# Attention's transposes placed one product later, the last means placed inside half products, and the last output pieces divided anew

## The reference, cut to what matters

```python
# NoPE differential attention: 4 heads, two 64-wide q/k maps each, 128-wide values
s = jnp.einsum('bqhcd,bkhcd->bhcqk', q, k).astype(jnp.float32)
s = jnp.where(mask, s, -jnp.inf)                  # block-causal mask, prompt only
p = jax.nn.softmax(s, axis=-1)
wdiff = p[:, :, 0] - lam * p[:, :, 1]
o = jnp.einsum('bhqk,bkhe->bqhe', wdiff, v)
yc = rmsnorm(o, da_g) * (1.0 - lam_init)
...
x = x + (jax.nn.silu(upc[..., :D_FF]) * upc[..., D_FF:]) @ w_dn    # D_FF = 2816
y = rmsnorm(x, norm_f)                                             # the output
```

## Time and profile before

| what | value |
|---|---|
| median of 3 runs | 1000.32 us (999.03 to 1001.5) |
| profiled execution, its own time | 1000.77 us |
| its span (first to last instruction and transfer) | 999.0 us |
| PE busy | 975.5 us (98%) |
| DVE busy | 692.0 us (69%) |
| ACT busy | 473.0 us (47%) |
| POOL busy | 161.2 us (16%) |
| mean granted TensorE clock | 0.996 |

### The profile page before, as it was taken

How to read it: one execution, slowest core, us unless ns; L and a number is a source line. 1 busy time by engine, 2 the same in 40 slices (tenths; PEclk the granted TensorE clock), 3 DMA queues, 4 the chain that set the end, 5 groups by cost and what they waited for, 6 DMA issues and landing times.

```text
span 999.0 us, 20129 instructions
## 1 busy us (share of the span) xinstructions
PE 975.5 (98%) x7763; PEld 952.6 (95%) x7763; DVE 692.0 (69%) x1161; ACT 473.0 (47%) x982; POOL 161.2 (16%) x343
## 2 busy tenths in 40 slices
PE   7999999999999998999999999999999999999996
PEld 6999899999999998999999999999999999999996
DVE  6887666687667898777775547777777777533353
ACT  5675555576555665655553433333333333322241
POOL 2000121110121221121112211111121111111000
PEclk9999999999999999999999999999999999999998
DMA  6522243364231222233244222222222223323342
GB/s 196 196 85 86 77 107 108 99 212 126 64 86 49 80 86 85 65 97 95 80 142 144 85 73 93 89 85 86 85 85 86 85 85 101 117 83 86 90 132 90
DMA packets 104086, 99.87 MB, mean 100 GB/s; under 512 B 4868, under 2 KB 99481, under 8 KB 103735
## 3 DMA queue, kind: packets, MB, share of 16 engines
q1 hardware_dynamic: 98799, 85.51, 28.0%
q10 hardware_dynamic: 4072, 10.23, 2.9%
q0 software_dynamic: 1120, 2.86, 1.0%
HBM read 91.26 MB, written 7.31 MB: 99 GB/s over the span
## 4 chain that ended last, share of the span: by engine, by line
PE 85%; DVE 6%; issue 4%; ACT 4%; POOL 1%; DMA 0%; DVEq 0%; POOLq 0%; ACTq 0%
PE D L1719 46%; PE D L1776 28%; PE D L1736 2%; DVE w_l L1305 2%; ACT w_h L1009 1%; PE X L1988 1%; PE X L2026 1%; PE D L1828 1%; PE D L1748 1%; DVE ups L1675 1%; PE D L1880 1%; PE X L1934 1%; DVE acc L1685 0%; PE X L1935 0%; PE X L1937 0%
## 5 line engine op out<-in xcount | busy, mean ns | idle before, releaser
L1305 DVE TENSOR_TENSOR w_l<-raw,w_h 128x512 fp32r<-128x512 f32 (+1 forms) x286 | 201.0, 720 | 111.2 <-ACT w_h L1009 109.4
L1776 PE MATMUL D<-a_h,w_h 128*128 128x272 f32 x840 | 250.4, 298 | 3.0 <-DVE tmp L1486 1.6
L1776 PE MATMUL D<-a_h,w_l 128*128 128x272 f32 x840 | 243.0, 289 | 0.0
L1776 PE MATMUL D<-a_l,w_h 128*128 128x272 f32 x840 | 241.6, 288 | 0.0
L1009 ACT ACTIVATE w_h<-raw 128x512 fp32r<-128x512 f32 (+1 forms) x286 | 171.5, 618 | 101.0 <-PE D L1719 77.8
L1776 PEld LDWEIGHTS D<-a_h,w_h 128*128 128x128 f32 x840 | 158.1, 188 | 8.4 <-DVE tmp L1486 3.0
L1776 PEld LDWEIGHTS D<-a_l,w_h 128*128 128x128 f32 x840 | 158.4, 189 | 0.0
L1776 PEld LDWEIGHTS D<-a_h,w_l 128*128 128x128 f32 x840 | 158.0, 188 | 0.0
L1719 PE MATMUL D<-h_h,w_h 128*128 128x272 f32 x704 | 145.9, 288 | 0.1
L1719 PE MATMUL D<-h_h,w_l 128*128 128x272 f32 x704 | 145.7, 288 | 0.0
L1719 PE MATMUL D<-h_l,w_h 128*128 128x272 f32 x704 | 145.1, 288 | 0.0
(11 more groups left out here) (346 smaller groups left out, 1676.8 us busy)
## 6 DMA issues: line engine op xcount, KB each, us to landing
raw<-in_w_in SPq DMA_DIRECT2D x64, 512.0 KB, 4.3
raw<-in_w_up SPq DMA_DIRECT2D x44, 512.0 KB, 4.3
raw<-in_w_down SPq DMA_DIRECT2D x20, 512.0 KB, 3.8
raw<-in_w_branch SPq DMA_DIRECT2D x12, 512.0 KB, 3.6
raw<-in_w_out SPq DMA_DIRECT2D x8, 512.0 KB, 4.2
raw<-in_w_down SPq DMA_DIRECT2D x10, 384.0 KB, 3.4
x_spill<-xT ACTq DMA_DIRECT2D x1, 2176.0 KB, 7.4
xT<-x_spill ACTq DMA_DIRECT2D x1, 2176.0 KB, 10.5
```

The lines of the kernel that those rows point to most:

```text
L1305: v.tensor_tensor(split_view(w_l, g), whole_view(g), split_view(w_h, g).bitcast(F32), ALU.subtract)\
L1776: last = t.matmul(out, wt[:, k, :], x[:, left, k, :], start=w in (1, 2, 5) and k == i == 0, stop=k == KQ - 1 and i == 2, skip_group_check= ...
```

## The change

Three edits.

1. In attention the sub-steps `t`, `wt`, `o`, `sq`, `rr`, `on`, `y`, `yt` and `yc` are filed one tick later. `s`, `mx`, `ex` and `wd` stay.
2. PE's mean 0 is issued in the middle of half block (6, 1), ahead of k tile 11 of 22, and mean 1 in the middle of half block (7, 1). DVE's two small steps of mean 1 stand behind the drain of (7, 1) now, no longer ahead of `scale` 0.
3. The last pieces: DVE scales rows c = 2 in two halves, the right half of rows c = 3, and the right half of the sample rows; ACT scales the left half of rows c = 3 and the left half of the sample rows. SP sends the first three, ACT the left half of c = 3 and the sample rows.

```diff
@@ -136,8 +136,8 @@
         at_time(time, *step)
     for u in range(17):
         t0, t1 = (99 + 28 * (x // 4) + (0, 5, 11, 18)[x % 4] if x >= 0 else 91 for x in (u - 1, u))
-        for dt, sub in ((0, "s"), (1, "mx"), (2, "ex"), (3, "wd"), (5.5, "t"), (6.5, "wt"), (8, "o"), (9, "sq"),
-                        (9, "rr"), (11.5, "on"), (t1 - t0 + 8, "y"), (t1 - t0 + 9, "yt"), (t1 - t0 + 9, "yc")):
+        for dt, sub in ((0, "s"), (1, "mx"), (2, "ex"), (3, "wd"), (6.5, "t"), (7.5, "wt"), (9, "o"), (10, "sq"),
+                        (10, "rr"), (12.5, "on"), (t1 - t0 + 9, "y"), (t1 - t0 + 10, "yt"), (t1 - t0 + 10, "yc")):
             if u or dt > 2:
                 at_time(t0 + dt, "at", sub, u)
 
@@ -229,9 +229,9 @@
     unit("mean", 0)
     unit("yTh", KD - 1, 0)
     unit("yTh", KD - 2, 1)
-    unit("mean", 1)
     unit("scale", 0)
     add("dnh", KD - 1, 1)
+    unit("mean", 1)
     unit("yTh", KD - 1, 1)
     unit("mean", 2)
     unit("scale", 1)
...
@@ scalar program
                 elif kind == "scale" and a[0] == 1:
-                    for i in range(2):
-                        cols = slice(DM // 2 * i, DM // 2 * (i + 1))
-                        sc.activation(yst[:, 3, cols], yst[:, 3, cols], ACT.Copy, scale=ssx[:, 3:4])\
-                            .then_inc(S["y_act"], 1)
-                        act.wait_ge(S["y_act"], i + 1)
-                        act.dma_start(y_p[0, 3 * P:4 * P, cols], yst[:, 3, cols]).then_inc(S["y_out"], 16)
+                    cols = slice(0, DM // 2)
+                    sc.activation(yst[:, 3, cols], yst[:, 3, cols], ACT.Copy, scale=ssx[:, 3:4]).then_inc(S["y_act"], 1)
+                    sc.activation(yst_s[0:TS, cols], yst_s[0:TS, cols], ACT.Copy, scale=ssx[0:TS, 4:5])\
+                        .then_inc(S["y_act"], 1)
+                    act.wait_ge(S["y_act"], 1)
+                    act.dma_start(y_p[0, 3 * P:4 * P, cols], yst[:, 3, cols]).then_inc(S["y_out"], 16)
+                    act.wait_ge(S["y_act"], 2)
+                    act.wait_ge(S["y_dve"], 6)
+                    act.dma_start(y_s[0], yst_s[0:TS, :]).then_inc(S["y_out"], 16)
@@ vector program
                     for c, cols in ((0, slice(0, DM)), (1, slice(0, DM))) if a[0] == 0 else \
-                            ((2, slice(0, DM // 2)), (2, slice(DM // 2, DM))):
+                            ((2, slice(0, DM // 2)), (2, slice(DM // 2, DM)), (3, slice(DM // 2, DM))):
                         v.tensor_scalar(yst[:, c, cols], yst[:, c, cols], ssx[:, c:c + 1], None, ALU.mult)\
                             .then_inc(S["y_dve"], 1)
                     if a[0]:
-                        v.tensor_scalar(yst_s[0:TS], yst_s[0:TS], ssx[0:TS, 4:5], None, ALU.mult).then_inc(S["y_dve"], 1)
+                        cols = slice(DM // 2, DM)
+                        v.tensor_scalar(yst_s[0:TS, cols], yst_s[0:TS, cols], ssx[0:TS, 4:5], None, ALU.mult)\
+                            .then_inc(S["y_dve"], 1)
@@ tensor program
+            def mean_of_halves(part):
+                pe.wait_ge(S["sq_added"], KD - 1 + KD - 2)
+                pe.wait_ge(S["sq_done"], KD + KD - 2 + 2 + (part + 1 if part else 0) - (part > 0))
+                out = D[:, (1, 3, 1)[part], :]
+                for c in HALF_TILES[min(part, 1)]:
+                    col, L = TILES[c]
+                    for i in ((0, 1, 2), (0, 1), (2,))[part]:
+                        source = (ssum[2][:], tmp_of(("sq", 2, KD - 2)), tmp_of(("sq", 2, KD - 1)))[i]
+                        last = t.matmul(out[0:L, c:c + 1], source[:, col:col + L], mean_w[:, 0:1],
+                                        start=i in (0, 2 * (part // 2)), stop=i == (2, 1, 2)[part])
+                last.then_inc(S["norm_mm"], 1)
             def spread_rstd(out, before, tiles):
...
                 elif kind == "dnh":
-                    product(n, g_h, g_l, halves=(a[1],), at_bank=0)
+                    half_means = (lambda k: mean_of_halves(a[0] - (KD - 2)) if k == JF // 2 else None) if a[1] else None
+                    product(n, g_h, g_l, half_means, halves=(a[1],), at_bank=0)
```

More of the change, by code:

```diff
@@ L781, in _ @@
             for i, (c, cols) in enumerate(((0, slice(0, DM)), (1, slice(0, DM)), (2, slice(0, DM // 2)),
-                                           (2, slice(DM // 2, DM)))):
+                                           (2, slice(DM // 2, DM)), (3, slice(DM // 2, DM)))):
                 sp.wait_ge(S["y_dve"], i + 1)
                 sp.dma_start(y_p[0, P * c:P * c + P, cols], yst[:, c, cols]).then_inc(S["y_out"], 16)
-            sp.wait_ge(S["y_dve"], 5)
-            sp.dma_start(y_s[0], yst_s[0:TS, :]).then_inc(S["y_out"], 16)
             sp.wait_ge(S["y_out"], 7 * 16)
@@ L1835, in _ @@
                     turn_over(9, banks(block_of[("if",)])[:, 0, :])
-                elif kind == "mean":
-                    pe.wait_ge(S["sq_added"], KD - 1 + KD - 2)
-                    pe.wait_ge(S["sq_done"], KD + KD - 2 + 2 + (a[0] + 1 if a[0] else 0) - (a[0] > 0))
-                    out = D[:, (1, 3, 1)[a[0]], :]
-                    for c in HALF_TILES[min(a[0], 1)]:
-                        col, L = TILES[c]
-                        for i in ((0, 1, 2), (0, 1), (2,))[a[0]]:
-                            source = (ssum[2][:], tmp_of(("sq", 2, KD - 2)), tmp_of(("sq", 2, KD - 1)))[i]
-                            last = t.matmul(out[0:L, c:c + 1], source[:, col:col + L], mean_w[:, 0:1],
-                                            start=i in (0, 2 * (a[0] // 2)), stop=i == (2, 1, 2)[a[0]])
-                    last.then_inc(S["norm_mm"], 1)
+                elif kind == "mean" and a[0] == 2:
+                    mean_of_halves(2)
                 elif kind == "mk" and a[0] == 0:
```

## The result

The change makes the kernel slower by a little: median 1001.8 us of 13 runs (1001.35 to 1003.4) against 999.22 us of 13 runs of the kernel before (998.56 to 1001.87), ratio 1.002 (1.0012 to 1.0028). That is within the 0.3% that the prediction counts as "same", but the whole interval lies above 1, so a small loss is shown. The forecast was 998.8, its range ended at 1001.0.

The account below looks back on a forecast made before the run. PE was taken as the bound, busy 975.5 of 999.0 us. Attention -0.3, means and clock -0.8 and last pieces -0.4 sum to -1.5 us, from the median 1000.32 to 998.8; eight in ten between 996.7 and 1001.0.

Parts of the forecast that it names:

- the sum of edit 1: Moving attention one product later: -0.5 us over PE's waits, lessened to -0.3; bounds -3.4 and +1.2.
- the first wait: PE's 1.14 us wait for `prob` ending at 345.23: 0.5 to 0.6 us gained, since PE then waits for DVE's drain.
- the second: PE's second `prob` wait in attention, the smaller part of 2.6 us: 0, within 0.5 either way.
- the third: PE's 0.9 us `prob` wait one head later: drain wait ends 0.6 us later, `wdT` wait shrinks by up to that; 0.
- for what is lost on the way: Allowance on the attention gain, lessening it from -0.5 to -0.3 us.
- rival (a): Attention's waits are gained whole: -3.4 us instead of -0.3, time 995.7 us; chance 0.14 with its partial forms.
- Rival (c): `y_tmp` and `junk` ahead of ACT's `w_h`: 0.59 us lost per place, 1003.5 us with eight places; chance 0.04.
- the cost: Means inside the half blocks: PE waits for the drain of (6, 1) between half blocks, 0.79 us lost.
- the credit: With the means apart, the clock stays up at the end: 1.6 us come back, -0.8 us for PE's part.
- rival (b): The clock falls again or the means weren't the reason: 1.6 us are missing, median 1000.4 us; chance 0.17.
- The ready time: At the end, pieces ready 1.7 us behind the scaling's start; ACT's queue issues 0.2 us earlier.
- the smaller last piece: The last transfer is 128 KB, not 256: 0.35 us at 370 GB/s, half of it taken.

Follow-up runs that it names:

- e10: The kernel before with edit 1 alone, for units 1 to 16 only: median 999.69 us, ratio 0.9985.
- e1: The change with unit 0's `t`, `wt`, `o`, `sq`, `rr` and `on` put back at their old ticks: median 999.41 us, ratio 0.9993.
- e8: The kernel before with only ACT's and POOL's attention steps of units 1 to 16 one tick later: median 1009.44 us, ratio 1.0094.
- e3: The kernel before with edit 2 alone (means 0 and 1 inside the half blocks): median 1000.2 us, ratio 1.0001.
- e2: The kernel before with edit 1 alone, unit 0 included: median 1002.18 us, ratio 1.002.
- e4: The kernel before with edit 3 alone (last pieces divided anew): median 1000.37 us, ratio 0.9997.
- e9: The kernel before with only `t` and `wt` of units 1 to 16 one tick later: median 1007.64 us, ratio 1.0078.
- e5: e1 with mean 0 back between the half blocks and mean 1 inside the last: median 998.14 us, ratio 0.9984.
- e6: e1 with the transposes of (7, 0) and (6, 1) issued inside half block (7, 1), at k tile 4: median 998.17 us, ratio 0.998.
- e7: The change with only `t` and `wt` of unit 0 moved back: median 1000.3 us, ratio 1.0004.
- e11: e5 with the attention group of units 1 to 16 two ticks later than in the kernel before: median 1004.11 us, ratio 1.0034.

## Why the prediction was wrong, point by point

**The step that failed is the sum of edit 1.** It looked for PE's waits and asked what becomes of each, in units 1 to 16. It took `t` to `yc` as a closed group that moves together. The group has two outside consumers, and both belong to unit 0: `s` of unit 1, which stays while `wt` of unit 0 moves, and the drain of the first output projection, which stays while `o` of unit 0 moves. In the kernel before neither shows as a wait of PE; the row that would have warned is DVE's, idle 4.63 us ahead of that drain. Forecast -0.3; measured by the trace +2.6 at unit 0 and -0.9 behind it, and by the runs at equal clock e10 -1.0 and the change less e1 +2.6 to +2.9. No rival named this.

**The waits of units 1 to 16: right in kind.** `prob` and `wdT` gone, 3.4 us; PE's waits for DVE's `tmp` up from 1.6 to 3.0, and DVE's `scb` and ACT's `tmp` new with 0.5 each. Unit 0's rows left out, 2.4 us came for 3.4 that went: -1.0, and PE's position says -0.9. Place by place: at the first wait 0.47 us for `scb` in place of 1.14 for `prob`, -0.67 where 0.5 to 0.6 was forecast, and by the mechanism forecast. At the second, near 380 us, 1.46 us of waits became 1.27, -0.2 where 0 was forecast. At the third, 395 to 407 us, 2.42 became 2.31, -0.1 where 0 was forecast: the 0.91 for `prob` became 1.50 for `tmp`, 0.6 more as forecast, and the 0.82 for `wdT` went. What was wrong is the step from -0.5 to -0.3 "for what is lost on the way": nothing was. -1.0 is three times -0.3, but nearer to it than to rival (a), -3.4.

**Rival (c), slower by ACT's order: not what happened.** ACT's order can cost (e8 +9.1 us by medians), but there it runs through `wdT` and the pair of `y` and `o`, which the change moves together, and not through `w_h`, as the rival had it. Where `w_h` did come later, at the third wait, it cost the 0.6 us forecast, in one place and not in eight.

**Edit 2: the cost right, the credit wrong.** The forecast cost was 0.79 us; the traces show 0.88 (e3 against e2), e3's runs 1.1. The idle time ahead of the three transposes is 0.61 for the forecast 0.8, the stretch between the half blocks 1.29 for 1.37. The slow clock cost 1.54 where it fell, for 1.6. (The half block of 8.33 us in the earlier trace rows is the one directly before, (6, 1), and not the one "two before it"; the comparison stands.) The clock stayed at 1.00 in the last two half blocks of the profiled execution. The second step that failed is in the total: the 1.6 us of slow clock were read from one profiled execution and credited to the median ("taken from the median, 1000.32 - 1.5"). Of the 13 runs of before beside the change seven lie within 998.5 to 999.3, where nothing is to be given back. The prediction named this as part of rival (b) ("The runs before spread by 2.5 us, which allows that not each of them lost it") and then gave it no weight in the sum. Against a run of before at full clock edit 2 is +0.9 to +1.1, not -0.8.

**The clock and what made it fall.** The trace supports the prediction's point that PE was busy and not idle when it fell. It does not support more: e2 and e4 have the same instructions there and opposite outcomes. That the means between the half blocks have a part in it is likely but not shown. Of six profiled executions that have both there, two fell behind them (before and e4, not e2, e8, e9, e10); of six that have one or none (change, e1, e3, e5, e6, e7) none did. Of all runs of the experiments 61 of 68 kept 0.997 or above with one or none, 47 of 119 with both (the change's runs are counted, e11's are not). But these numbers also hold the other place, near 115 us, described at the end, and for a run without a profile it is not on record where its clock fell. The Trainium skill, "TensorE: Matmul & The Clock Gate", section "What's actually happening", has the half rate as the state of an idle array. The e4 window, 8.00 of 8.00 us busy at 0.80, disagrees.

**Edit 3: right sign, size -0.2 to -0.3 for -0.4.** The ready time came as worked out (1.75 us for 1.7), which gave 0.15 for 0.2. The share taken for the smaller last piece, half of 0.35, came out as 0.1: from the last issue to the end of the span it was 4.14 us before and 4.04 in the change. The spread of such executions, 0.1, is as large, so which of the two bounds is nearer isn't shown.

**The sum as it should have been, at full clock:** from 999.1 of before, -1.0 for units 1 to 16 (e10), +1.1 for edit 2 (e3) and -0.3 for the pieces (e4) make 998.9; e1, which has just these, measured 998.9 to 999.1. Unit 0 adds 2.6 to 2.9: 1001.8. The runs of before that lost clock then bring its median up to 999.22, and the ratio down to 1.002.

## What to carry to other kernels

When a group of steps is moved and its first and last instances are special, list for each step of every instance the waits on its semaphores that lie outside the group, and look at who stands in front of them; a wait of zero length before the change is no row of any view, and the slack it had is read from the idle time of its neighbours (here DVE's 4.63 us). A move is paid or earned by the group: where the whole gains 1 us, a part of it lost eight here. And before slow-clock time is credited to a change, see in how many of the runs it is there at all: the granted clock beside each run's time tells it.

## What the runs showed of the hardware

- **One program, three times.** The kernel before takes 999.1, about 1000.9 or about 1001.7 us, at mean granted clocks of 0.997 to 0.998, 0.996 and 0.994, on the same chip and in turn. The steps answer to two places where the clock falls in some executions only. One is behind the means at 980 us (the profiled execution of before, 0.996). The other lies near 115 us, ahead of attention, where the change edits nothing (e1 0.996; e2, e8 and e10 0.995). e4's profiled execution has both falls and 0.994. Windows near 115 us of the change, where it did not fall, and of e1, where it did:

```profile
105.00:125.00 20.00, 20.00 (x152) 17.59 (x152) 11.57 (x25) 9.91 (x26) 4.39 (x6) 1.00 0.25 71
```

```profile
105.00:125.00 20.00, 20.00 (x140) 17.59 (x140) 11.56 (x25) 8.91 (x24) 4.32 (x6) 0.91 0.17 47
```

  PE is busy for all of the 20 us in both, and issues 12 matmuls less in the second. Ahead of the fall it does short matmuls of the mLSTM branch's sample rows, 110.08 to 113.84 in the change; in e1 the 2 us from 114 on are at 0.56. What decides between them no run here tells. Nor do the runs tell why this fall is in six of the 13 profiled executions (e1, e2, e4, e8, e10, e11) and in none of the others.
- **One mean and the transposes kept the clock.** e5 still has mean 0 and the five transposes in a row between two half blocks, and its window shows 1.00:

```profile
976.00:978.00 2.00, 2.00 (x21) 1.99 (x20) 1.39 (x4) 0.84 (x2) 0.33 (x1) 1.00 0.00 0
```

  Ten of its 11 runs were at 0.997 or above. In e11 it fell during 6.04 us of idle time and was at 0.50 in the 3 us behind. There the rule of the idle array fits (the Trainium skill, "TensorE: Matmul & The Clock Gate", section "What's actually happening"), as it doesn't at 980 us.
